# Cached values two turns nearer to their keys, and the last feed-forward unit in quarters with the final norm in halves

## The reference

```python
x = x + 0.5 * swiglu(rmsnorm(x, norm_ffn1), ffn1_w_in, ffn1_w_out)
m, k, v, logf, s = token_mix(rmsnorm(x, norm_mix), ...)   # hgrn2 heads and forgetting attention
x = x + m
x = x + 0.5 * swiglu(rmsnorm(x, norm_ffn2), ffn2_w_in, ffn2_w_out)
y = rmsnorm(x, norm_final)

def fox_decode(q, k, v, logf, k_past, v_past, logf_past):   # for each sample sequence, 8 heads of 64
    s_past = q @ k_past.T + cq + suffix                     # 2048 cached keys
    s_new = q @ k.T + cq - cq.T, causal                     # the 4 new keys
    p = softmax(concat([s_past, s_new]))
    return p[..., :2048] @ v_past + p[..., 2048:] @ v
```

## Time and profile before

| | |
|---|---|
| median of 3 runs | 1293.64 us (1292.74 to 1295.45) |
| the profiled execution's own time | 1294.23 us |
| its span, first to last instruction | 1292.3 us |
| mean granted TensorE clock | 0.994 |
| PE busy | 1261.5 us, 98% |
| DVE, ACT, POOL busy | 589.4, 474.8, 110.4 us |
| read and written in HBM | 162.19 MB and 8.93 MB |
| the mix's turns, in the trace | about 589 to 834 us |
| the last unit of the second feed-forward | ends at about 1277.6 us |

### The profile page before, as it was taken

One profiled execution on the slowest core, in us unless ns is written; L12 is line 12 of the kernel. 1 busy time (PEld: TensorE's weight loads), 2 busy tenths in 40 slices (PEclk: granted clock), 3 DMA queues, 4 the chain that ended last, 5 costly groups with the idle time before them and its releaser, 6 DMA issues.

```text
span 1292.3 us, 29960 instructions
## 1 busy us (share of the span) xinstructions
PE 1261.5 (98%) x12437; PEld 1180.6 (91%) x12437; DVE 589.4 (46%) x1096; ACT 474.8 (37%) x765; POOL 110.4 (9%) x247
## 2 busy tenths in 40 slices
PE   9999999999999999998898999999999999999997
PEld 8999999999999999996555666699999999999997
DVE  6644332244354433236765676645443521343433
ACT  6543221122233112434867777543222310222222
POOL 1000000000013000000223522122000000000000
PEclk9999999999999999999989999999999999999999
DMA  8323422232322352355699999333323322323301
GB/s 202 98 82 81 144 85 65 65 95 67 122 90 66 117 144 65 115 177 163 239 370 324 342 343 360 133 99 84 98 79 114 103 77 65 96 66 105 112 11 70
DMA packets 186649, 172.35 MB, mean 133 GB/s; under 512 B 11393, under 2 KB 149154, under 8 KB 186562
## 3 DMA queue, kind: packets, MB, share of 16 engines
q1 hardware_dynamic: 185394, 167.47, 41.2%
q0 software_dynamic: 1104, 3.67, 0.8%
q10 hardware_dynamic: 64, 0.02, 0.0%
HBM read 162.19 MB, written 8.93 MB: 132 GB/s over the span
## 4 chain that ended last, share of the span: by engine, by line
PE 91%; DVE 4%; issue 2%; ACT 2%; DMA 1%; SPq 0%; ACTq 0%; DVEq 0%
PE ps L2156 78%; PE ps L989 2%; PE ps L1074 2%; PE ps L1089 2%; PE ps L914 1%; DMA d_keys<-in_cache_k 1%; PE ps L954 1%; PE ps L934 1%; ACT d_keysT L1334 1%; PE ps L752 0%; PE ps L2296 0%; DMA gain_rows<-in_norm_final 0%; PE ps L895 0%; PE ps L2310 0%; DVE ps L1791 0%
## 5 line engine op out<-in xcount | busy, mean ns | idle before, releaser
L2156 PE MATMUL ps<-n_hi,w_hi 128*128 128x272 f32 x1856 | 387.1, 288 | 2.0 <-DVE w_lo L2626 0.8
L2156 PE MATMUL ps<-n_hi,w_lo 128*128 128x272 f32 x1856 | 386.8, 288 | 0.0
L2156 PE MATMUL ps<-n_lo,w_hi 128*128 128x272 f32 x1856 | 385.2, 288 | 0.0
L2346 ACT ACTIVATE w_hi<-w_raw 128x2048 fp32r<-128x2048 f32 (+2 forms) x76 | 156.0, 2052 | 540.7 <-PE ps L2156 540.6
L2156 PEld LDWEIGHTS ps<-n_hi,w_hi 128*128 128x128 f32 x1856 | 292.9, 188 | 2.7 <-issue 2.5
L2156 PEld LDWEIGHTS ps<-n_lo,w_hi 128*128 128x128 f32 x1856 | 292.7, 189 | 0.0
L2156 PEld LDWEIGHTS ps<-n_hi,w_lo 128*128 128x128 f32 x1856 | 290.7, 189 | 0.0
L2500 DVE TENSOR_TENSOR w_lo<-w_raw,w_hi 128x2048 fp32r<-128x2048 f32 (+2 forms) x75 | 191.6, 2555 | 49.5 <-ACT w_hi L2346 49.5
L2156 PE MATMUL ps<-g_hi,w_lo 128*128 128x272 f32 x704 | 145.7, 288 | 0.0
L2156 PE MATMUL ps<-g_hi,w_hi 128*128 128x272 f32 x704 | 145.5, 288 | 0.0
L2156 PE MATMUL ps<-g_lo,w_hi 128*128 128x272 f32 x704 | 145.2, 288 | 0.0
(11 more groups left out here) (360 smaller groups left out, 1230.4 us busy)
## 6 DMA issues: line engine op xcount, KB each, us to landing
w_raw<-in_ffn_w_in SPq DMA_DIRECT2D x87, 512.0 KB, 4.9
d_keys<-in_cache_k SPq DMA_DIRECT2D x128, 256.0 KB, 5.3
d_values<-in_cache_v SPq DMA_DIRECT2D x124, 256.0 KB, 6.1
w_raw<-in_w_in_mix SPq DMA_DIRECT2D x28, 512.0 KB, 4.7
w_raw<-in_ffn_w_out SPq DMA_DIRECT2D x16, 768.0 KB, 5.5
w_raw<-in_ffn_w_out SPq DMA_DIRECT2D x16, 640.0 KB, 4.8
w_raw<-in_w_out_mix SPq DMA_DIRECT2D x8, 512.0 KB, 4.9
suffix_scratch<-d_log_f_sums SPq DMA_DIRECT2D x32, 64.0 KB, 2.1
```

Of the source, the lines that this page charges most:

```text
L2156: mm = pe.matmul(bank(4 * j + 2 * t + half), wp, xp[:, k, half * HALF:(half + 1) * HALF], start=(k == 0 and wp is w[0] and xp is x_hi), st ...
L2346: nc.scalar.activation(w_hi[j][:, 0:kt * UC], w_raw[j][:, 0:kt * UC], ACT.Copy).then_inc(w_hi_ready, 1)
```

## The change

In the mix the value pairs of a sequence move two turns earlier: half 0 to 8b+7 to 8b+10 and half 1 to 8b+11 to 8b+14; the last sequence's half 0 takes one pair in each of the turns 63 to 66, its half 1 stays at 67 and 68. The steps before and behind them move too: the transposes of the first half's probabilities and ACT's copy of them from i = 7 to i = 6, the copies out to 8b+13 and 8b+16 (68 and 69 for the last one), the weighting to 8b+19 (67 and 70 stay for the last two), and the exponential of the factor and its addition on DVE from i = 4 to i = 3. In a turn that has the first pair of a half, the pair's product comes after both parts of the scores and not between them. The product with the new tokens' values comes with another pair (`NEW_AT`).

At the end the last unit is made in quarters: first half of the tokens for both feature tiles, then the second half, with a signal after each quarter. Adding to x, squares, gains and sums of squares follow by quarters. The sums over features for token tiles 0 and 1 are made by PE before the last quarter, and their 1/rms by ACT and DVE meanwhile; those of tiles 2 to 4 behind the last quarter. The transposes go token tile by token tile, ACT makes six of the ten copies out (both of tile 1), DVE four, and the sample tokens' rows are stored by one DMA instead of two.

```diff
         def value_turn(b, half, k):
             if b == DB - 1:
-                return 8 * b + (9 if half == 0 else 11) + k // 2
-            return 8 * b + (9 if half == 0 else 13) + k
+                return 8 * b + (7 + k if half == 0 else 11 + k // 2)
+            return 8 * b + (7 if half == 0 else 11) + k
         VALUE_PAIRS = sorted(((b, half, k) for b in range(DB) for half in range(2) for k in range(4)),
                              key=lambda v: (value_turn(*v), v))
...
             r = RING_PAIRS.index(w)
             return d_v[r % V_RING], dv_landed[r % V_RING], 32 * (r // V_RING + 1)
+        NEW_AT = [(0, 1, 1)] + [(b, 0, 3) for b in range(1, DB)]
+
         def values_through(b, half):
-            return 2 * VALUE_PAIRS.index((b, half, 3)) + 2
+            last = NEW_AT[b] if half == 0 else (b, 1, 3)
+            return 2 * VALUE_PAIRS.index(last) + 2
         def keys_copied(x):
...
                     mm = pe.matmul(ps[0:NR, B_M, M_NEW:M_NEW + NS], d_q[b % 2][:, j * NR:(j + 1) * NR],
                                    pT[:, T_FK + j, SEQ:T], start=(j == 0), stop=(j == NJ - 1), skip_group_check=True)
                 mm.then_inc(new_done, 1)
-            if i == 7 and b < DB:
+            if i == 6 and b < DB:
                 pe.wait_ge(dexp[0], 2 * b + 2)
                 if b == 1:
                     pe.wait_ge(pt_copied[1], 1)
...
                                            stop=True, skip_group_check=True)
                     mm.then_inc(oT_done, 1)
-        OUT_AT = [8 * b + 22 for b in range(DB - 2)] + [67, 70]
+        OUT_AT = [8 * b + 19 for b in range(DB - 1)] + [70]
         def products_tensor(pe, x):
...
                 pe.matmul(ps[:, B_O, :], d_pTn[b % 2][:, :], d_vn[:, :], start=False, stop=False, skip_group_check=True)
             for w, (b, half, k) in values_of(x):
-                if half == 0 and k == 3:
+                if (b, half, k) == NEW_AT[b]:
                     new_values(b)
             y = x - 1
             active = 0 <= y < 2 * DB * SETS
...
                 if i % 4 == 0 and b:
                     pe.wait_ge(dexp[i // 4], 2 * b if i == 0 else b)
                 scores(y, 0)
-            for w, (b, half, k) in values_of(x):
-                values(w, b, half, k)
+            due = values_of(x)
+            late = any(k == 0 for _, (b, half, k) in due)
+            if not late:
+                for w, (b, half, k) in due:
+                    values(w, b, half, k)
             if active:
                 scores(y, 1)
+            if late:
+                for w, (b, half, k) in due:
+                    values(w, b, half, k)
         def mix_tensor(pe, gated_product):
             pe.wait_ge(drained, 2 * P_MIX_OUT)
...
                 for half in range(2):
                     if x == COPY_AT[c][half]:
                         copy_out(c, half)
-            if i == 7 and b < DB:
+            if i == 6 and b < DB:
                 copy_probsT(b, 0)
             if i == 2 and 1 <= b <= DB:
                 copy_probsT(b - 1, 1)
             if i == 3 and b + 1 < DB:
                 query(b + 1)
-            if i == 4 and 1 <= b <= DB:
+            if i == 3 and 1 <= b <= DB:
                 act.wait_ge(dd_step, b)
                 nc.scalar.activation(d_sm[:, 3:4], d_sm[:, 2:3], ACT.Exp, scale=-1.0).then_inc(de_done, 1)
-        COPY_AT = [(8 * b + 15, 8 * b + 17) for b in range(DB - 1)] + [(67, 69)]
+        COPY_AT = [(8 * b + 13, 8 * b + 16) for b in range(DB - 1)] + [(68, 69)]
         def forget_scalar(act, x):
             if x == 0:
...
                                         ALU.add).then_inc(sn_done, 1)
                 dve.wait_ge(sn_done, b + 1)
                 nc.vector.tensor_reduce(d_mx[0:NR, 1:2], d_pn[:, :], AX_X, ALU.max).then_inc(snm_done, 1)
-            if i == 4 and 1 <= b <= DB:
+            if i == 3 and 1 <= b <= DB:
                 dve.wait_ge(group_max, 10 * b)
                 nc.vector.tensor_tensor(d_sm[:, 2:3], d_sm[:, 1:2], d_all[0][:, :], ALU.add)\
                     .then_inc(dd_step, 1)
...
                 for j in range(2):
                     load_columns(P_MIX_OUT + i, i * 2 + j, j, io["w_out_mix"], 0, KD)
             ffn_loads(P_FFN[1], io["ffn2_w_in"], io["ffn2_w_out"], False)
...
+            for i in range(TT):
+                dst = y_prompt[0, i * P:(i + 1) * P, :]
                 for q in range(2):
                     half = slice(q * 512, (q + 1) * 512)
...
+                    if q == 0 or i == 1:
+                        sp.wait_ge(y_copied[0], (1, 2, 4, 5)[i] + q)
+                    else:
+                        sp.wait_ge(y_copied[1], max(i, 1))
                     sp.dma_start(dst[:, half], y_nat[Y_ROWS[i], i, half]).then_inc(y_stored, 16)
...
+            sp.wait_ge(y_copied[0], 6)
+            sp.wait_ge(y_copied[1], 4)
+            sp.dma_start(y_sample.rearrange("b t d -> (b t) d"), y_nat[Y_ROWS[TT], TT, :]).then_inc(y_stored, 16)
+            sp.wait_ge(y_stored, 16 * (2 * TT + 1))
             mix_stores_waited(sp)
...
                 unit(p0, 1, KD, x_hi, x_lo, first=(p0 == 0), middle=None if stage else lambda: sum_squares(1),
                      second_tile=lambda: pe.wait_ge(ms_ready, stage + 1))
+            def column_sums(out, tiles):
+                for i in tiles:
+                    mm = pe.matmul(out[:, i:i + 1], sumsq[:, Y_COLS[i]], ones[:, 0:1], start=True, stop=True,
+                                   skip_group_check=True)
+                mm.then_inc(ss_done, 1)
+
+            def last_unit(pair, kt, x_hi, x_lo):
+
+                pe.wait_ge(w_hi_ready, 2 * pair + 2)
+                pe.wait_ge(w_lo_ready, 2 * pair + 2)
+                pe.wait_ge(drained, 2 * pair)
+                for half in range(2):
+                    for t in range(2):
+                        if (half, t) == (1, 1):
+                            pe.wait_ge(sq_summed, TAIL_SUM + 2)
+                            column_sums(ps[:, 4, :], range(2))
+                        for k in range(kt):
+                            mm = products(1, kt, t, k, (half,), x_hi, x_lo)
+                        mm.then_inc(mm_done, 1)
+
             def ffn(f, p0, stage):
                 done = f * KF
                 for c, (kt, pairs) in enumerate(zip(CHUNKS, (IN_A, IN_B))):
...
                         if k == 0 or k == kt - 2:
                             pe.wait_ge(g_ready, done - 2 if k == 0 else done)
-                    with pe.Fori(0, KD // 4) as i:
+                    end = f == 1 and c == 1
+                    with pe.Fori(0, KD // 4 - 1 if end else KD // 4) as i:
                         for j in range(2):
                             unit(i + p0, j, kt, g_hi[f], g_lo[f], g_wait)
                     p0 += KD // 4
+                    if end:
+                        unit(p0 - 1, 0, kt, g_hi[f], g_lo[f])
+                        last_unit(p0 - 1, kt, g_hi[f], g_lo[f])
             ffn(0, P_FFN[0], 0)
             first_pair(P_MIX_IN, 1, n_hi[0], n_lo[0])
...
...
+            def tile_transposes(i):
+                for q in range(2):
+                    transposes(i, q, range(4 * q, 4 * q + 4)).then_inc(yt_done[q], 1)
+
             pe.wait_ge(drained, units - 1)
...
+            pe.wait_ge(xg_ready, 8)
+            tile_transposes(0)
+            pe.wait_ge(sq_summed, TAIL_SUM + 4)
+            column_sums(ps[:, 6, :], range(2, TT + 1))
+            tile_transposes(1)
             pe.wait_ge(ms_ready, 4)
...
+            pe.wait_ge(x_ready, TAIL_X + 4)
+            pe.wait_ge(xg_ready, 10)
+            tile_transposes(2)
+            pe.wait_ge(ms_ready, 5)
+            tile_transposes(3)
+            pe.wait_ge(y_copied[0], 1)
+            pe.wait_ge(y_copied[1], 1)
+            tile_transposes(TT)
         @block.scalar
...
                     split_hi(P_MIX_OUT + i + 1, j, KD)
                     next_input(2, 2 * (2 * i + j))
             ffn(1, P_FFN[1], 2)
-            act.wait_ge(ms_ready, 4)
-            nc.scalar.activation(y_root[:, :], y_ms[:, :], ACT.Sqrt).then_inc(root_ready, 1)
-            act.wait_ge(rstd_step, 13)
-            for i in range(TT + 1):
-                act.wait_ge(yt_done[0], i + 1)
-                nc.scalar.activation(y_nat[Y_ROWS[i], i, 0:512], ps[Y_ROWS[i], 2 * (i % TT), :], ACT.Copy,
+            def tail_square(t, half):
+                cols = slice(half * HALF, (half + 1) * HALF)
+                d = KD - 2 + t
+                act.wait_ge(x_ready, TAIL_X + 2 * half + t + 1)
+                nc.scalar.activation(x_sq[1][:, d, cols], xT[:, d, cols], ACT.Square).then_inc(x_squared, 1)
+                nc.scalar.activation(x_gained[:, d, cols], xT[:, d, cols], ACT.Copy, scale=gains[:, 3, d:d + 1])\
+                    .then_inc(xg_ready, 1)
+
+            def token_root(n, tiles):
+                act.wait_ge(ms_ready, 4 + n)
+                nc.scalar.activation(y_root[:, tiles], y_ms[:, tiles], ACT.Sqrt).then_inc(root_ready, 1)
+
+            def y_copy(i, q):
```

(56 more changed lines are left out.)

54 lines of the change are left out of this document (9 added, 45 removed).

## The result

The changed kernel takes 1301.16 us (median of 5 runs), the kernel before 1293.64. The ratio is 1.0053, with a 95% interval from 1.0039 to 1.0067. The forecast was 1288.3 us, faster. The profiled execution of the changed kernel took 1300.25 us, its span is 1298.3 us, 6.0 more than before. Two of the twelve executions of the kernel of experiment 7 ran at a mean granted clock of 0.65 and took 1719 us; they are not in its ratio.

A forecast was written before the change was run, and what follows sets the result against it. PE bounds the kernel (91% of the chain), with transfers nearly full in the mix. Mix -1.9 and end -3.4 sum to -5.3: 1294.23 becomes 1288.9, and the median, 0.6 lower, 1288.3 us; range 1284.5 to 1292.0.

The forecast's parts named there:

- No product is added or removed: Mix: value pairs only change turns; the two early pairs fit into PE's wait at turn 9, cost 0, at most 1.8 us.
- a pair behind both parts of the scores costs what it costs between them: 0: Mix, order inside a turn: issuing a value pair after both score parts instead of between them adds 0 us.
- The early transposes: Mix, turns 8b+6: PE waits for exponentials, covered except in sequence 3, none from sequence 4; +0.95 us, bounds 0 to 3.3.
- The copies out: Mix, ACT's queue: a 0.59 us copy leaves i = 1 for i = 5, ending PE's wait at turn 27; -0.6 us.
- Where ACT has slack except for sequences 1 and 2: Mix, i = 5: ACT can take the moved copy out; sequences 1 and 2 counted within the early transposes' nets.
- The loads: Mix: value lead stays six turns; waits for keys at turns 18 and 20, 1.87 and 1.22 us, stay in place.
- Rival D: Mix: key waits shrink as 1 MB of values moves before them, and a low clock goes; 1284 us, chance 10%.
- The end of the mix: From turn 65: 1.0 from less PE work, 1.0 from waits at turns 69 and 70; -2.0 us, bounds -0.5 and -3.1.
- The end of the program: Behind the last unit: 14.7 us becomes 10.8, plus 0.5 of sums ahead; -3.4 us, bounds -4.0 and -2.1.
- E: Time mark: PE's last product, 1277.6 before; forecast first store 2.4, last store 8.2 and end 10.8 us after it.
- The drain of 1.38 us: End, ACT's table load for Sqrt: the skill's drain, 2.66 us in all, would make the sum -4.5 instead of -5.3.
- A: Rival, mix: early transposes' waits stay uncovered and drop the clock; mix +5.7, total +2.3, 1296 us, slower, chance 6%.

The follow-up runs named there:

- experiment 7: New end on the kernel before, old value turns, but the last sequence's pairs spread so that turn 67 alternates two pairs of each half: ratio 0.9972.
- experiment 6: Changed kernel with value pairs back at their old turns and between the scores, other moves and new end kept: 1294.24 us, ratio 0.9996.
- Experiment 1: Kernel before with only the PSUM strips exchanged, so value products write the rows that the same turn's scores write: 1319.47 us, one run.

## Why the prediction was wrong

**What failed: the price of a moved pair.** The step "No product is added or removed" and, in the copies' part, "a pair behind both parts of the scores costs what it costs between them: 0" put the moved products at nothing. They cost 19.4 us of PE in the turns 1 to 62. PE's idle time gave 6.8 us back, and the mix alone came out 11.3 us slower where -1.9 was forecast. Taking only the value pairs back to their old turns and order gives 7.4 us of that back (experiment 6). Experiment 1 shows the cause by itself: 25 us for the strips and nothing else. The evidence stood in the trace of before: a pair alone cost 0.9 us, and 56 pairs beside the scores cost next to nothing, since the products of a turn with scores alone (1 to 8) took 0.7 to 1.1 us and those of most turns with both 0.9 to 1.1. I had taken 0.9 us as what a pair costs everywhere, and did not ask why the sum of the turn was smaller than its parts.

**The early transposes.** The waits came where the prediction put them: 1.25, 1.31 and 0.97 us at turns 14, 22 and 30 (1.25, 1.19 and 1.0 forecast), none from sequence 4 on, and 0.43 at turn 6. With the new end and the weighting at 8b+19 alone they were covered even better than forecast (0.1 us late at turn 51, 0.95 forecast, by one trace). Yet that edit cost 3.1 us (0.9995 against 0.9971). No step of the prediction has a term for it. The stops for instructions are part of what the trace shows there, but where the 3.1 us come from is open.

**The copies out.** Forecast -0.6 for turn 27. Measured +6.1 without the early transposes (with the factor and the weighting moved too), 0 on top of them. The wait at turn 27 did not go by it: 1.84 us in that kernel, 1.82 before. In the changed kernel it is 0.78. "Where ACT has slack except for sequences 1 and 2" named the place of some 2 us of the loss (turns 15 and 23) and then did not price it.

**The loads.** I left the waits for keys at turns 18 and 20 where they were; they are gone in the changed kernel, because a PE slowed by collisions comes later. Experiment 1, where only the strips differ, has lost them too. It is part of what the longer products got back from the waits. Rival D had forecast these waits to shrink, for another reason, and with a gain.

**The end of the mix.** From turn 63 to the transposes of the prompt's last results 29.4 us pass, 30.7 before: -1.3, where -2.0 was forecast. The idle time before the weighting at turn 70 was to vanish; 0.47 of its 0.77 us are left.

**The end of the program.** -3.4 forecast, -3.75 measured (intervals allow 2.2 to 5.2). The 0.5 us of sums and the first store at E+2.3 (2.4 forecast) are as forecast, the last store at E+7.2 comes a microsecond sooner than forecast (8.2), and the end at E+10.4 (10.8). The clock held 1.00, so the transposes took 0.115 us each and not a mix of 0.117 and 0.19. The table load took 1.28 us and the next function began 0.01 us behind it, and Sqrt ran before the last product. The drain of 1.38 us that the Trainium skill, ScalarE: Activation LUTs, gives in "What ACT_TABLE_LOAD costs" does not show in this trace either.

**The sum.** End -3.75, early transposes, copies, factor and weighting +3.2, value turns +7.4: +6.9 us, which is the ratio 1.0053. These three are differences along one line of kernels, so they add up by construction; the separate measurement of the mix, +11.3, agrees with +10.6 for its two parts. The miss is not luck or noise: the forecast for the end was met, and the whole of the error lies in the mix. Of the rivals, A forecast slower, but by low clocks after waits; the clock was 1.00. The rival that I needed, products that no longer run side by side, was not on the list.

## What to carry to other kernels

Before a product is moved to another place, read what runs beside it and which rows of PSUM each writes: narrow products on different strips share the array, and one moved next to its own strip costs its whole time (here 0.85 us a turn) with no wait to show for it. If the parts of a turn add up to more than the turn, something runs in parallel, and its condition is part of the price. And split a change of two independent halves: here one was worth 3.75 us and the other lost 11. The same holds for an experiment: the edit of the early transposes also moved the weighting, and so its 3 us have two possible owners.
